# Retention decay factors in a fused four-layer block: the exponential one beat after its arguments, the diagonal's doubling two beats after

## The reference, cut to what matters

```python
diff = pos[:, None] - pos[None, :]
decay_mat = jnp.where(diff >= 0, jnp.exp(lg[:, None, None] * jnp.maximum(diff, 0.0)), 0.0)
inner = jnp.einsum('bhid,bhjd->bhij', qc, kc) * decay_mat
```

## Time and profile before

| | us |
|---|---|
| median of 3 runs | 1060.45 |
| lowest and highest run | 1054.36, 1062.51 |
| the profiled execution's own time | 1062.14 |
| its span, first to last instruction | 1060.3 |
| mean granted TensorE clock | 0.952 of full |
| busy over the span: TensorE, VectorE, ScalarE, GpSimd | 89%, 66%, 45%, 6% |

### The profile page before, as it was taken

One profiled execution on the slowest core, in us unless ns is written; L12 is line 12 of the kernel. 1 busy time (PEld: TensorE's weight loads), 2 busy tenths in 40 slices (PEclk: granted clock), 3 DMA queues, 4 the chain that ended last, 5 costly groups with the idle time before them and its releaser, 6 DMA issues. The chain is left out here.

```text
span 1060.3 us, 14368 instructions
## 1 busy us (share of the span) xinstructions
PE 946.7 (89%) x5572; PEld 820.6 (77%) x5572; DVE 702.9 (66%) x1058; ACT 475.7 (45%) x800; POOL 66.7 (6%) x63
## 2 busy tenths in 40 slices
PE   4999987999798899999999897987789679999996
PEld 3788866989676778888879676775578579999885
DVE  4567878878777745667686766647745657755643
ACT  4455554544333336555555434434543434333541
POOL 0201110000000010101010000100000000000000
PEclk9999998999899889999999989989999879999999
DMA  7544456665566354545454664341222326663660
GB/s 261 168 150 159 142 177 193 206 225 170 197 216 205 122 187 148 181 158 180 158 187 154 219 227 145 103 158 57 80 80 80 130 89 239 238 199 120 221 215 40
DMA packets 89348, 174.55 MB, mean 165 GB/s; under 512 B 4269, under 2 KB 8770, under 8 KB 89282
## 3 DMA queue, kind: packets, MB, share of 16 engines
q1 hardware_dynamic: 86656, 166.78, 47.1%
q0 software_dynamic: 1888, 6.25, 1.8%
q10 hardware_dynamic: 738, 0.61, 0.2%
HBM read 172.57 MB, written 1.06 MB: 164 GB/s over the span
## 5 line engine op out<-in xcount | busy, mean ns | idle before, releaser
L1570 DVE TENSOR_TENSOR wlo<-raw,whi 128x1024 fp32r<-128x1024 f32 (+2 forms) x278 | 323.5, 1177 | 164.2 <-ACT whi L1287 163.3
L1287 ACT CAST whi<-raw 128x1024 fp32r<-128x1024 f32 (+2 forms) x278 | 276.5, 1010 | 203.6 <-PE acc L987 73.6
L996 PE MATMUL acc<-xhi,whi 128*128 128x256 f32 x736 | 215.1, 292 | 9.6 <-DVE slo L1588 4.5
L997 PE MATMUL acc<-xhi,wlo 128*128 128x256 f32 x736 | 210.1, 285 | 0.0
L998 PE MATMUL acc<-xlo,whi 128*128 128x256 f32 x736 | 210.0, 285 | 0.0
L985 PE MATMUL acc<-whi,xhi 128*128 128x512 f32 (+2 forms) x368 | 151.3, 411 | 11.9 <-DVE xlo L1588 4.6
L996 PEld LDWEIGHTS acc<-xhi,whi 128*128 128x128 f32 x736 | 143.0, 194 | 13.0 <-issue 5.3
L987 PE MATMUL acc<-whi,xlo 128*128 128x512 f32 (+2 forms) x368 | 144.5, 393 | 0.0
L986 PE MATMUL acc<-wlo,xhi 128*128 128x512 f32 (+2 forms) x368 | 144.3, 392 | 0.0
L997 PEld LDWEIGHTS acc<-xhi,wlo 128*128 128x128 f32 x736 | 143.2, 195 | 0.7 <-issue 0.5
L998 PEld LDWEIGHTS acc<-xlo,whi 128*128 128x128 f32 x736 | 143.0, 194 | 0.0
(11 more groups left out here) (291 smaller groups left out, 1179.1 us busy)
## 6 DMA issues: line engine op xcount, KB each, us to landing
raw<-in_e_w_in SPq DMA_DIRECT2D x28, 1024.0 KB, 5.3
raw<-in_o_w_in SPq DMA_DIRECT2D x28, 1024.0 KB, 5.1
raw<-in_w_mod SPq DMA_DIRECT2D x24, 1024.0 KB, 5.1
raw<-in_w_ffn_in SPq DMA_DIRECT2D x20, 1024.0 KB, 5.5
raw<-in_w_in SPq DMA_DIRECT2D x14, 1024.0 KB, 5.2
raw<-in_w_ffn_out SPq DMA_DIRECT2D x10, 1024.0 KB, 5.1
raw<-in_e_w_out SPq DMA_DIRECT2D x8, 1024.0 KB, 6.0
raw<-in_o_w_out SPq DMA_DIRECT2D x8, 1024.0 KB, 5.2
```

The lines of the kernel that those rows point to most:

```text
L996: mm(o, wh, hi, start=a, stop=False, skip_group_check=True)
L997: mm(o, wl, hi, start=False, stop=False, skip_group_check=True)
L1287: nc.scalar.copy(whi[:, s.i % SPLIT_SLOTS, 0:s.nk, 0:n], raw[:, s.raw.i % RAW_SLOTS, s.koff:s.koff + s.nk, 0:n]).then_inc(S["hi_ready"], 1)
L1570: tt(wlo[:, slot, 0:s.nk, 0:n], raw[:, s.raw.i % RAW_SLOTS, s.koff:s.koff + s.nk, 0:n], whi[:, slot, 0:s.nk, 0:n].bitcast(F32), ALU.subtra ...
```

## The change

The step `ret_decay` is divided into `ret_arg` (VectorE) and `ret_exp` (ScalarE). Their instructions are the same as before. Beat n now has, in this order, the doubling of head n-2, the arguments of head n and the exponential of head n-1. The sequence takes ten beats in place of nine. The three kinds are added to `PASSABLE`.

```diff
-    def decay(h):
-        if h > 0:
-            pl.tick(pl.step("ret_two", h=h - 1), "m_ready")
-        if h < 8:
-            pl.tick(pl.step("ret_decay", h=h, after=side_done), "m_arg", "m_exp")
+    def decay(n):
+        if n >= 2:
+            pl.tick(pl.step("ret_two", h=n - 2), "m_ready")
+        if n < 8:
+            pl.tick(pl.step("ret_arg", h=n, after=side_done), "m_arg")
+        if 1 <= n < 9:
+            pl.tick(pl.step("ret_exp", h=n - 1), "m_exp")
...
-    for h in range(9):
-        pl.at(pl.pos + 2 + h, lambda h=h: decay(h), 1)
+    for n in range(10):
+        pl.at(pl.pos + 2 + n, lambda n=n: decay(n), 1)
...
-            "evac_conv_z", "qkT", "scores", "PT", "pv", "oT", "forget_rows", "mod", "mod_out", "load", "g_q", "gqa_kT", "g_scores", "g_exps", "g_norm", "g_PT", "g_pv")
+            "evac_conv_z", "qkT", "scores", "PT", "pv", "oT", "forget_rows", "mod", "mod_out", "load", "g_q", "gqa_kT", "g_scores", "g_exps", "g_norm", "g_PT", "g_pv", "ret_arg", "ret_exp", "ret_two")
...
-            def ret_decay(st):
-                wait(("m_arg", st.on["m_arg"]))
+            def ret_exp(st):
+                wait(("m_arg", st.h + 1))
                 f(ret_d[:, st.h, :], ret_d[:, st.h, :], ACT.Exp)
                 f(ret_m[:, st.h, :, :], ret_m[:, st.h, :, :], ACT.Exp).then_inc(S["m_exp"], 1)
...
-            def ret_decay(st):
+            def ret_arg(st):
                 h = st.h
                 dve.wait_ge(S["loaded_ret"], 16)
```

More of the change, by code:

```diff
@@ L1503, in _ @@
                     "evac_ctxkv": evac_kv, "evac_latkv": evac_kv, "gqa_kT": gqa_kT, "ret_T": ret_T,
-                    "ret_T2": ret_T2, "ret_decay": ret_decay, "ret_pv": ret_pv, "ret_norm": ret_norm, "ret_out": ret_out,
+                    "ret_T2": ret_T2, "ret_exp": ret_exp, "ret_pv": ret_pv, "ret_norm": ret_norm, "ret_out": ret_out,
                     "evac_mix": evac_mix, "evac_ffb": evac_ffb}
@@ L2019, in _ @@
                     "g_scores": g_scores, "g_norm": g_norm, "g_pv": g_pv,
-                    "ctx_state": ctx_state, "ret_q": ret_q, "ret_decay": ret_decay, "ret_two": ret_two, "ret_scores": ret_scores,
+                    "ctx_state": ctx_state, "ret_q": ret_q, "ret_arg": ret_arg, "ret_two": ret_two, "ret_scores": ret_scores,
                     "ret_norm": ret_norm, "ret_out": ret_out, "evac_mix": evac_mix, "post": post, "evac_ffb": evac_ffb}
```

## The result

The changed kernel's median over its first four runs is 1041.77 us (1041.06 to 1043.93), that of the kernel before in the same comparison 1058.78 us (1054.36 to 1062.51): a ratio of 0.984, 95% interval 0.9817 to 0.9863. The same changed kernel was run twice more: 0.9901 (0.9868 to 0.9934) and 0.9861 (0.9836 to 0.9885). The mean of the three is about 0.987, some 14 us.

A forecast was written before the change was run, and what follows sets the result against it. Waits between engines were taken to bound the attention stage, TensorE what follows. Beats 0 and 1 win 2.97 us, beats 2 to 7 10.2, together 13.2; 1062.14 - 13.2 = 1048.9 us, range 1044 to 1056.

The forecast's parts named there:

- The mechanism: Grouped-attention stage: ScalarE's wait for arguments goes, VectorE is late next; a plain beat falls 1.70 us, from 7.62 to 5.92.
- the anchor of the sum: The profiled execution's own time, 1062.14 us, from which 13.2 us were taken; the runs' median was 1.7 lower.
- item 5: Beat 1: rotary half held by matmuls ending 720.86, so 1.07 us won, then 1.70 and 0.20; 2.97 together with beat 0.
- What went at nothing: Last doubling, last exponential (0.52 us if its cover were gone), `PASSABLE` (at most 2 us) and weight loads: no cost counted.
- the signs of failure: Exponentials 6.5 us or more apart with maximum or L1443 waits, stage clock below 0.9, or a later stretch growing.
- item 6: Stage exit: beats 2 to 7 win 10.2 us, last subtraction 13.2 early, beat 8's copy of part 1 13.3 early.
- Shifts the outcome by 2 or so: Whole-kernel time: allowance in us for the three runs before lying 8 us apart.
- Hidden anyway: Rival in the stage: TensorE's chain re-forms, beats stay near 7.6 us, time 1062; less than 6 us won, chance 0.08.
- The clock bites: Rival in the stage: TensorE's clock loss costs 3.5 us, 9.7 won, 1052.4 us; chance 0.17 together with TensorE's chain.
- Slower by the clock: Rival: stage falls to 1.2 GHz; at a share of 0.6 eight beats cost 12.7 us more, 1074.8; chance 0.05.
- Retention and what follows move forward as they are: Behind the stage: retention and feed-forward, bound by TensorE, keep their order and length and start 13.2 us earlier.
- the ring: One stage beat's ScalarE and VectorE chain, from exponentials through arguments, cast, subtraction and maximum to next exponentials: 7.62 us before.

## Why the prediction was right and wrong

The mechanism was right and so were most of its terms; two terms were not, the anchor of the sum and item 5. The wait of ScalarE and the eight waits of VectorE for the cast are gone; VectorE is late next; a plain beat is 5.91 to 5.93 us (5.92 was forecast) and each beat but beat 1 wins 1.69 to 1.72 (1.70). TensorE's beat is 5.83 to 5.90 where nothing else binds (5.75 to 5.95). What went at nothing shows no cost either: `PASSABLE` was run by itself, and for the last doubling, the last exponential and the weights (DMA share 0.23, 0.22 was expected) the exit comes as early as the beats say. The cast L1445, named among the signs of failure, never held up the exponentials of the changed kernel.

The step of the mechanism that failed is item 5. It had beat 1 win 1.07 up to the reciprocal, on the ground that the rotary half waits for the matmuls that end at 720.86. Those matmuls aren't the sub it waits for. In the order of the list the sub of beat 1 stands in front of the scores of beat 1, and in the kernel before these start at 716.38:

```profile
715.94 0.39 PE L987 MATMUL acc<-whi,xlo 128*128 128x512 f32 x1
...
716.38 1.13 PE L1138 MATMUL spsum<-ptb,sidef 64*128 64x512 f32 x4
```

So the sub that counts had ended at 716.33, over five us before the half, and the matmuls from 717.85 to 720.86 are the next panel's. The half of 721.98 shows no idle time in front of it: it waited for no matmul, only for VectorE's own order. In the changed kernel it (715.59) starts right behind the maximum, while such matmuls run:

```profile
714.45 1.21 DVE L1751 TENSOR_REDUCE nmx<-spsum 128x2 f32<-128x1024 f32 x1
...
715.59 0.41 DVE L1878 TENSOR_TENSOR g<-acc,g 128x256 f32<-128x256 f32 x1
...
715.77 0.39 PE L989 MATMUL acc<-whi,xlo 128*128 128x512 f32 x1
```

Beat 1 wins 1.90, that is 1.70 and the 0.20 of the doubling. With it the items give 1.71 + 1.90 + 6 x 1.70 = 13.8 on VectorE. By the way of item 6, on ScalarE, they give 1.71 + 1.90 + 5 x 1.70 = 12.11 to the last exponentials (12.14 measured), and the copy behind them comes 3.28 and not 774.78 - 769.68 = 5.10 us later: 13.93 together. Measured are 13.96, 13.93 and 13.97 in the three profiles of the changed kernel against the first of the kernel before. Item 5 cost 0.6 to 0.8 us.

What cost more was the anchor. The sum was made against the profiled execution's own 1062.14 us, and that is a high one of the kernel before, whose median is 1058.78 in the same comparison and 1058.70 over nineteen runs in a later one. The prediction did say that the median of its three runs gives 1047.3, and took 1048.9 all the same. From 1048.9 down to 1041.77 it is 7.1 us: 3.4 are the anchor (1062.14 - 1058.78), 0.8 the stage (13.96 - 13.2, item 5), and 3.0 the amount by which the medians of the first comparison lie further apart (17.0) than the stage explains (14.0). The range allowed 4.9 below the forecast. Anchor and item 5 used up 4.2 of it, and the 3.0 did the rest; without the anchor's 3.4 the time would have been inside, and without the 3.0 too.

The 3.0 are the luck of four runs, as far as the record shows: the 14 runs of the changed kernel have a median of 1045.2 us, inside the range, and six of them lie below 1044. "Shifts the outcome by 2 or so" was too little for three or four runs of a program whose runs lie 8 us apart. With the later median and the right sum the forecast is 1058.7 - 14.0 = 1044.7, and the second and third median, 1046.16 and 1045.70, lie 1.0 to 1.5 above it.

The rivals. "Hidden anyway" is refuted: the occupancy of ScalarE was the lowest of three, and taking a wait off it won 14 us, because the other two stood behind that engine's order. The prediction tied this rival to a rule of the Trainium skill (Perfetto Trace Analysis, Identifying the Most-Contended Engine). The section does say to optimise the engine with the highest occupancy first. That a wait taken off another engine is then worth nothing is the prediction's own step, and it is this step that the runs refute. The section also judges TensorE's headroom by its weight loads and not by the busy time of its matmuls: that is 31.29 / 58.61 = 0.53 in the earlier trace rows, which leaves VectorE with 0.70 as the most occupied engine, and its 12.9 us of waits for the cast lead to the very place that was changed.

"The clock bites" did not come about: no stretch at 1.2 GHz fell into the changed stage in any of the three profiles (granted clock 1.00), so what one would cost there was not measured. "Slower by the clock" is refuted: TensorE was busier, and its clock in the stage was higher than before.

"Retention and what follows move forward as they are" is right to 0.05 us up to the retention's end. From there on equal kernels differ by a step of 1.6 us, and the shorter stretches of the two kernels (74.67 and 72.83) lie 1.8 apart, which is the wait at the stage's exit (5.10 - 3.28) that item 6 counts.

## What to carry to other kernels

An instruction that waits for a result nobody needs yet costs what stands behind it in its engine's order, not what the engine idles; so look at what is queued behind the wait, and move either the waiter one turn later or the important work in front of it. The start-to-start times of one turn of the ring, and the end of the engine that becomes late next, gave the gain of a turn to 0.02 us before anything was run, in all beats but the one where the wrong matmuls were taken for a bound. A forecast of a time should start from the median of the runs and not from the profiled one. Before saying which matmuls an evacuation waits for, find them by the order of the list and not by what runs next to it in time.

## What the runs showed that was not expected

A stage bound by waits repeats to a few hundredths: seven beats of 55.01, 55.05, 55.04 us and of 42.87, 42.90, 42.86 (the last two on different chips), while whole runs of the same kernels lie up to 9 us apart. Behind the stage the difference is a step of 1.6 us for one more stretch at 1.2 GHz; in front of it 5 us were seen that the clock alone doesn't give. A change of 1 us, which the rounds used here did not show in the medians, is read off such a stage at once; and the medians of four runs each can be 4 us apart for the same kernel.
